# A chunked two-way recurrence on one core: units of 128 tokens taken in two serial steps of 64, with 64x64 products and two inverse levels

## What is computed

```
def step(S, inp):
    r_t, w_t, k_t, v_t, a_t, b_t = inp
    sa = jnp.einsum('bhvk,bhk->bhv', S, a_t)
    S = S * w_t[:, :, None, :] + sa[..., None] * b_t[:, :, None, :] + v_t[..., None] * k_t[:, :, None, :]
    return S, jnp.einsum('bhvk,bhk->bhv', S, r_t)
s_final, y = lax.scan(step, s0, (r, w, k, v, a, b), reverse=reverse)
```

## Times and profile before

| | us |
|---|---|
| median of 3 runs | 2692.49 |
| lowest, highest | 2692.34, 2693.08 |
| the profiled execution: span of core 0 | 2688.9 |
| TensorE busy | 2568.6 (96%) |
| VectorE busy | 1872.8 (70%) |
| GpSimd busy | 1188.7 (44%) |
| ScalarE busy | 1081.2 (40%) |

### The profile page before, as it was taken

One profiled execution on the slowest core, in us unless ns is written; L12 is line 12 of the kernel. 1 busy time (PEld: TensorE's weight loads), 2 busy tenths in 40 slices (PEclk: granted clock), 3 DMA queues, 4 the chain that ended last, 5 costly groups with the idle time before them and its releaser, 6 DMA issues.

```text
span 2688.9 us, 67501 instructions
## 1 busy us (share of the span) xinstructions
PE 2568.6 (96%) x28608; PEld 2413.9 (90%) x28608; DVE 1872.8 (70%) x2978; ACT 1081.2 (40%) x1978; POOL 1188.7 (44%) x1154
## 2 busy tenths in 40 slices
PE   4899999999999998999999998999799999999998
PEld 3899999999999996777777777999799999999998
DVE  3365675856758565787666657799778678677686
ACT  3434243342433422433333333443453453443534
POOL 1323232322323225555555545656446556565662
PEclk8999999999999999999999998999899999999999
DMA  8333425334254364445454456453223332333231
GB/s 325 106 102 118 140 71 186 113 111 140 80 175 123 101 203 116 131 133 149 142 155 139 145 162 181 133 179 98 61 63 86 81 101 63 87 82 100 63 79 71
DMA packets 282409, 329.10 MB, mean 122 GB/s; under 512 B 76288, under 2 KB 215936, under 8 KB 273536
## 3 DMA queue, kind: packets, MB, share of 16 engines
q1 hardware_dynamic: 274448, 278.66, 33.4%
q0 software_dynamic: 5904, 39.32, 6.9%
q10 hardware_dynamic: 1760, 6.82, 0.6%
HBM read 221.83 MB, written 91.36 MB: 116 GB/s over the span
## 4 chain that ended last, share of the span: by engine, by line
PE 85%; DVE 8%; issue 2%; ACT 2%; DMA 2%; SPq 1%; POOL 0%; DVEq 0%; ACTq 0%; POOLq 0%
PE ser L972 18%; PE gbank L972 13%; PE inv L972 11%; PE bank L972 11%; PE gbank L1416 8%; PE inv L1416 8%; PE ser L1416 7%; PE bank L1416 7%; DVE a_sum L2323 1%; DMA ring<-in_wblocks 1%; PE inv L1174 1%; DVE a_sum L2327 1%; PE bank L1157 1%; DVE a_sum L2331 1%; DVE a_lo L2297 1%
## 5 line engine op out<-in xcount | busy, mean ns | idle before, releaser
L954 POOL TENSOR_TENSOR w_lo<-raw_w,w_hi 128x512 fp32r<-128x512 f32 x264 | 427.3, 1632 | 366.9 <-ACT w_hi L1756 366.9
L849 POOL TENSOR_TENSOR wsp<-ring,wsp 128x1024 fp32r<-128x1024 f32 x67 | 205.2, 3063 | 653.9 <-ACT wsp L1518 653.9
L1756 ACT ACTIVATE w_hi<-raw_w 128x512 fp32r<-128x512 f32 x264 | 165.2, 633 | 261.6 <-PE ser L1416 98.4
L972 PE MATMUL ser<-xn_hi,wsp 128*128 128x384 f32 x816 | 217.1, 339 | 6.0 <-POOL xn_lo L855 6.0
L1416 PE MATMUL gbank<-a_hi,w_hi 128*128 128x288 f32 x616 | 185.8, 302 | 30.8 <-POOL w_lo L954 14.6
L972 PE MATMUL gbank<-xn_hi,wsp 128*128 128x384 f32 x800 | 212.6, 339 | 0.3 <-issue 0.3
L972 PE MATMUL bank<-xn_hi,wsp 128*128 128x384 f32 x800 | 210.2, 337 | 0.5 <-issue 0.5
L972 PE MATMUL inv<-xn_hi,wsp 128*128 128x384 f32 x800 | 210.4, 338 | 0.0
L2126 DVE TENSOR_TENSOR gmat<-gbank,gmask 128x1024 f32<-128x1024 f32 x144 | 175.6, 1219 | 43.8 <-PE gbank L972 43.0
L1742 ACT ACTIVATE a_hi<-a_sum 128x1152 fp32r<-128x1152 f32 x88 | 103.0, 1172 | 224.5 <-DVE a_sum L2331 78.6
L972 PE MATMUL gbank<-ub 64*64 64x128 f32 (+1 forms) x3456 | 179.4, 310 | 9.0 <-DVE gmat L2126 7.6
(11 more groups left out here) (402 smaller groups left out, 7541.1 us busy)
## 6 DMA issues: line engine op xcount, KB each, us to landing
ring<-in_wblocks SPq DMA_DIRECT2D x107, 512.0 KB, 5.3
ub<-op_d SPq DMA_DIRECT2D x144, 256.0 KB, 2.8
raw_w<-in_wquads SPq DMA_DIRECT2D x33, 1024.0 KB, 4.8
raw_w<-in_wquads POOLq DMA_DIRECT2D x22, 1024.0 KB, 9.5
op_d<-ar SPq DMA_DIRECT2D x32, 576.0 KB, 5.4
op_d<-bk SPq DMA_DIRECT2D x32, 576.0 KB, 6.2
raw_w<-in_wquads SPq DMA_DIRECT2D x44, 256.0 KB, 3.7
raw_w<-zsum POOLq DMA_DIRECT2D x11, 1024.0 KB, 13.1
```

The costliest lines, as they stand in the source:

```text
L849: GT(wsp[s % 2][1][:], ring[(N_ADA_RING + s) % RING][:], wsp[s % 2][0][:].bitcast(F32), ALU.subtract).then_inc(S["wsplit_lo"], 1)
L954: GT(w_lo[n % 4][:], src, w_hi[n % 4][:].bitcast(F32), ALU.subtract).then_inc(S["wl_ok"], 1)
L972: return nc.tensor.matmul(out, lhsT, rhs, start=start, stop=stop)
L1756: A(w_hi[s][:], raw_of(op)[:, m, :].rearrange("p (k c) -> p k c", k=KH), ACT.Copy).then_inc(S["wh_ok"], 1)
```

## The change

Each unit of 128 tokens is handled as two sub-chunks of 64 (`SC`, `NS` = 18 per direction), one after the other:

- the decays are summed, centred and stored per 64 tokens (`decay_sums`: 18 scans of 64 for 9 of 128; `mid`, `emid`, `gstep` twice as long);
- the grams are formed within 64 tokens only: per direction 64 columns for the first two masks' parts and 128 for the last two, in half of each bank, with one masking instruction of 512 columns instead of 1024;
- the inverse stops at blocks of 64: LEVELS = 5, two levels in flight, no `last_blocks`; `ltc` is one GpSimd instruction and `tt` one, instead of two and four;
- the serial part is done twice a unit, k = 0 and 1: `ur_keys` (once, both k) and `ur_state`, `serial_u`, `serial_s`, `y_state`, `serial_y` (each per k), all on 64x64 quarters; direction 1 takes the halves in the other order (`side`), so at each step the two directions sit in different halves of the partitions;
- `ur_out`, `u_out` and `carried` run twice a unit, `carried` now on ScalarE; `states` twice on VectorE;
- look-ahead of the gram is 3 units instead of 4, `gmat` has four buffers instead of five; `ur` and `u` get a bank pair of their own (`su`), the transposed operands share bank 0 with the gram, the finished chunks' products move into `gbank` and `inv`;
- the last `serial_y` of a unit is issued in the next iteration, after its first `ur_state`.

The core of the diff:

```diff
-LEVELS = 6
+LEVELS = 5
+AHEAD = 3
+def side(d, k):
+
+    return k if d == 0 else 1 - k

+            def ur_keys(u):
+                pe.wait_ge(S["gram_ok"], 2 * u + 2)
+                if u:
+                    pe.wait_ge(S["u_ok"], 2 * u)
+                order = (1, 0) if j == NC_LAT else (0, 1)
+                for k in order:
+                    for d in range(2):
+                        b = halves_of[side(d, k)]
+                        for h in range(2):
+                            ins = smm(su[halves_of[side(d, k) ^ h], h, UR[k]:UR[k] + HD], g[b, d, h, 2, :], vb[q][b, d, halves_of[h]], k == order[0])
+            def serial_u(u, k):
+
+                pe.wait_ge(S["tri_ok"], u + 1)
+                pe.wait_ge(S["ur_ok"], 2 * u + k + 1)
+                for d in range(2):
+                    x = side(d, k)
+                    for h in range(2):
+                        b = halves_of[x ^ h]
+                        ins = smm(su[halves_of[x], h, UU[k]:UU[k] + HD], tt[u % 2][b, d, h, :], ur[b, h, :], False)
+                for x in (1, 0):
+                    if x == 0:
+                        pe.wait_ge(S["u_ok"], 2 * u + k + 1)
+            def y_state(u, k):
+                if k:
+                    pe.wait_ge(S["yh_full"], u + 1)
```

TensorE's loop after the change, and the parts of the other loops that its steps meet:

```diff
+                if serial:
+                    ur_keys(s)
                 if inverses:
                     turn(s)
+                if serial:
+                    ur_state(s, 0)
+                if there(s - 1):
+                    serial_y(s - 1, 1)
+                if ahead:
+                    gram(s + AHEAD, 0)
+                if serial:
+                    serial_u(s, 0)
+                if inverses:
+                    left(s)
+                if serial:
+                    serial_s(s, 0)
+                if ahead:
+                    gram(s + AHEAD, 1)
+                if serial:
+                    ur_state(s, 1)
+                    y_state(s, 0)
...
+                for x in finals(s - 1):
+                    gate(*x)
+                    spread(*x)
+                if inverses:
+                    right(s)
+                if serial:
+                    serial_y(s, 0)
+                    serial_u(s, 1)
+                    y_state(s, 1)
...
+                for x in finals(s):
+                    variance(*x)
                 if there(s + 1):
                     token_major(s + 1)
                 if serial:
+                    serial_s(s, 1)
```

619 lines of the change are left out of this document (312 added, 307 removed).

## The result

The changed kernel takes 2715.3 us (median of 4 runs, 2712.3 to 2722.4) against 2692.8 us of the kernel before beside it: ratio 1.0086, 95% interval 1.0071 to 1.0101. It is slower by 0.9%; the prediction said 3.1% faster, with 2662 as its upper end. The profiled execution took 2712.3 us, with a span of 2710.5, 21.6 us more than before.

What follows compares the result with a forecast made beforehand. The prediction took TensorE's full queue as the bound: -145 queue, +62 stops, +12 small inversion, -2 modulation, -11 run-up, together -84, span 2605 from 2688.9. Median forecast 2608 us (-3.1%), range 2552 to 2662.

Steps and rivals of the forecast that it cites:

- TensorE's queue: Array work per recurrence unit, counted in rounds of products: 2.04 us less a unit, -145 us over 71 units.
- the stops: TensorE standing between links of the serial chain for lack of covering work: 0.88 us a unit, +62 us in all.
- the walk: Pass through a unit's new order, link by link, for uncovered waits: 0.30, 0.32, 0.20 and 0.06 us.
- the modulation: Modulation products of eight pairs in the recurrence: they hide a stop each and keep their cost, -2 us.
- Run-up: From the first gram to the first use of a state: 10.4 us instead of 21.7, -11 us.
- Small inversion: Units 9 to 23, its VectorE work coming ahead of both states: 0.8 us a unit, +12 us.
- Stop at the copy of up: Between serial_u 0 and serial_s 0, 0.47 us of work covers a link of 0.81: a stop of 0.30 us.
- Dense stages: Stages outside the recurrence: no change expected; a change of more than a few us would fail the prediction.
- Four abreast: Rival: ur_keys and serial_u rounds writing one bank run one half at a time, +33 us, 2641; chance 0.07.
- The clock's rival: Rival: stops put recurrence units at the lower clock, 4.3 us each; half the units gives 2763; chance 0.05.
- The chain: Rival: half the cover in a unit is late, stops reach 1.75 us a unit, +62 us, 2670; chance 0.14.
- It doesn't shorten TensorE's queue at all, the new instructions having a floor of their own: Rival: the recurrence's smaller products save no TensorE time, about 2692 + 5; chance 0.04.

Runs made afterwards that it cites:

- e6_long_ur: The changed kernel with ScalarE's two copies of ur a unit writing their values three times: 2723.7 us, ratio 1.0129 to the kernel before.
- e4_before_noblocks: The kernel before, leaving out from the second unit on the gram blocks that its mask sets to zero, same instruction count: 2677.5 us, ratio 0.9964.
- e3_few_loads: The changed kernel with loads of operands and values cut to 8 columns from unit 7 on: 2693.8 us, ratio 1.0014 to the kernel before.
- e2_tiny64: The changed kernel with 16 more products a unit of two columns each (64 instructions) in ur_keys: 2780.7 us, ratio 1.0341 to the kernel before.
- e5_wide64: The changed kernel with 16 more products a unit of 256 columns each (64 instructions) in ur_keys: 2802.0 us, ratio 1.0399 to the kernel before.
- e7_no_values: The changed kernel without the values' part of y within a step and of the state's update: 2687.5 us, ratio 0.9968 to the kernel before.
- e9_before_tiny64: The kernel before with 16 more two-column products a unit (64 instructions) behind serial_ur: 2759.6 us, ratio 1.0264.
- e17_348: The changed kernel without 14 of 16 serial_y products, the state update's values' part and gram part 1, from the second unit: 2630.6 us, ratio 0.9777.

## Why the prediction was wrong, point by point

- **The failed step is the conclusion on what bounds the kernel**: "what is taken off that queue shortens the unit, until the serial chain through ScalarE and VectorE shows". There is a third limit besides TensorE's array and the chain, the supply of TensorE's instructions, and no term of the sum and no rival had it. The prediction counted rounds of four quarters, and so took 8 records of 128 columns made into 16 of 64 for half the work. In instructions it is more work: 411 a unit became 468. The block of 256, which lasted 5.1 us (8.025 us for 403), would last 4.0 us, and each then stalls 0.66 us: +78 us on the recurrence. The one number that would have raised the question was on the page of before, 228 packets of instructions for 57216 records. The count is not the whole of it: the next packet also starts later in after, 1.9 us after the crossing in the median for 1.2 in before. With 1.1 us for the packet and 1.4 behind it this is 4.4 us for 3.7, and by before's 3.7 a block of 4.0 us would mostly have been in time. Traffic isn't the reason (with the DMA engines under half busy it is 1.6 for 1.1 us), and which property of the new order it is stays open.
- The Trainium skill bears on this, Runtime: NRT & Kernel Launch, Instruction fetch mechanics: an engine's instruction store is a queue refilled in 16 KiB blocks of 256 instructions, the next block being fetched while the current one runs. The trace agrees with the block (4.00 MB in 244 packets) and with one block ahead. The same section says that the fetch is mostly hidden, since dispatch is slower than the refill; here the measurement decides, and it was not hidden: 84 us in 71 units.
- **TensorE's queue, -2.04 us a unit, and the stops, +0.88**: together -1.16; own time fell by 0.75, and by some 0.87 with the clock's share taken out. In the plainest units, at the first, sixth and seventh place of a pair, own time has a median of 6.58, 6.66 and 6.70 us (forecast 6.96 as a mean over all units). What the walk missed is in the units around the modulation products and in the one that starts a new pair's states. Medians of own time by place in the pair are -1.17, -0.92, -0.97, -0.47, -0.66, -1.17, -1.13, -1.22 and -0.37 us against before. So in four of nine places the unit fell as forecast; the three small ones are the fourth, the fifth and the last. The waits shown above name candidates: mrow, ScalarE's copy of the modulation products, which gram 0 waits for since both use one bank (5.0 us, 7 times), and VectorE's states (5.0, 6 times). The prediction gave the modulation "-2 us" in a clause. Of the 0.41 x 71 = 29 us by which own time missed, the +12 and -2 of the sum had allowed for 10 and the clock took some 8 more than in before; the other 11 or so belong to that term and to the unit at the end of a pair, which no experiment tested one by one.
- **Single terms.** Run-up -9.3 for -11 (from the first gram to the first use of a state 13.7 us, 10 to 12 forecast). A unit takes 8.47 us, above the 7.8 that the prediction had named as its failure. Small inversion: units 9 to 23 have 7.61 us of own time and the others 7.19, +0.42 for the +0.8 forecast. In before the same units had +0.27, so the change added 0.15 x 15 = 2 us, not 12. Stop at the copy of up: there at step 0, 0.05 us behind the copy. Dense stages: no change in the first, and see the sum for the rest.
- **VectorE's mask** of 512 columns was put at 0.69 us by even cost per column; groups by line of the changed kernel, 1040 to 1600 us:

```profile
L2202 DVE TENSOR_TENSOR gmat<-gbank,gmask 128x512 f32<-128x512 f32 x131 | 90.5, 691 | 63.7 <-PE gbank L1162 61.6
```

- **Rivals.** Four abreast holds: the 16 records of ur_keys, which write one bank from both row halves, take 0.397 us up to the first transpose, 0.23 and a change of form; one half at a time they would need 0.46 and the change. The clock's rival came true in a small part that nothing in the sum had: 20.5 us of the recurrence at the lower level, about 9 us of time, not half the units. (The 4.3 us a unit that it was priced at don't follow from its two rows either; 6 us of queue at 0.43 for 0.28 is 3.2 more.) The chain was not the bound (e6_long_ur). "It doesn't shorten TensorE's queue at all, the new instructions having a floor of their own" was the nearest in kind and was dismissed because rounds of 64 columns already go at 0.058 us. That row was right for 16 records, and says nothing of 256.
- **Sum**: forecast for the 71 units were -145 + 62 + 12 - 2 = -73 us; own time gave -53 and the stalls +78, so they account for 20 (some 8 of it the clock) and 78 us of the error. The run-up is 2 us off, and from the last unit's first copy to the end of the span it is now 1085.8 us for 1079.9, 6 more, with the second step of the last unit in it. 2605 + 20 + 78 + 2 + 6 = 2711; the span is 2710.5.

## What to carry to other kernels

Count instructions as well as columns: work out from the trace how long TensorE takes for 256 of its instructions (weight loads, matmuls, waits; an fp32 product is four), and if a change brings that near 4 to 5 us, expect part or all of what smaller products save to be lost again in stops. A stop called "issue" in the middle of a group with all its operands there, coming again every 256 instructions, is this limit; the queue of instructions on the page has the count. Then cut columns where the instructions stay (as in e4_before_noblocks) or join products, and look at own time and stalls apart. Before comparing the own times of two kernels, compare their time at the lower clock: here it made kernels with different work look alike.

## What the runs showed of the hardware that I had not expected

- TensorE's instructions arrive in packets of 16384 bytes, 256 instructions. In after the next packet starts 1.4 to 3.1 us after the last crossing, takes 1.1 us, and TensorE can use it 1.4 us after its landing. Stalled blocks were 3.9 to 5.5 us apart in after (10th to 90th percentile).
- The packet starts later under other DMA traffic: 2.3 us with the DMA engines over 80% busy, 1.6 under 50%. With the loads of e3_few_loads cut, the median of all packets fell from 1.91 to 1.61.
- The granted clock was lower where TensorE had more stops or fewer columns; which of the two it goes by wasn't separated. Averaged over the span, the executions of before were granted 0.978 to 0.987, those of after 0.969 to 0.978, of e2_tiny64 (64 more instructions, hardly any columns) 0.959 to 0.970, and of e5_wide64 (as many instructions, 256 columns wide) 0.980 to 0.985 again.
- A product's own issue: 64 more instructions cost 0.51 us of own time a unit on quarters, about 0.34 of it (5 ns each) without the clock's share, and 0.87 us (13.6 ns each) in the 128*64 form, at two columns.
- **Left open**: the stalls don't go by the mean length of a block alone. e7_no_values has blocks of 4.6 us and stalls 0.52 us in each, e9_before_tiny64 blocks of 4.9 us and 0.09; e17_348 has 5.2 us and 0.23, before 5.1 and 0.06. In before and its descendants the packet starts after some 70 instructions of the block (1.2 to 1.3 us), in after and its descendants after some 120 to 145 (1.6 to 2.4 us). What triggers the fetch was not found; the more uneven order of after, in which dense groups follow waits, is an argument and not shown.
